# Chunk-loop stores of h2 and of the residual move from the sync queue to GpSimd's, in a one-core hybrid mLSTM and convolution layer

## The reference

```python
def step(carry, xs):                    # one chunk of 128 tokens, 4 heads
    C, n, m = carry
    ...
    P = jnp.einsum("bhld,bhsd->bhls", qc, kc) * jnp.exp(D - m_row[..., None])
    num = w_inter[..., None] * jnp.einsum("bhld,bhde->bhle", qc, C) + jnp.einsum("bhls,bhse->bhle", P, vc)
    den = w_inter * jnp.einsum("bhld,bhd->bhl", qc, n) + jnp.sum(P, axis=-1)
    h = num / jnp.maximum(jnp.abs(den), jnp.exp(-m_row))[..., None]
    ...
y = jnp.einsum("bse,ed->bsd", jnp.concatenate([y_mlstm, y_conv], axis=-1), w_out[layer])
x = x + rms_norm(y, post_mix_norm_w[layer])
h2 = rms_norm(x, pre_mlp_norm_w[layer])
a = jax.nn.relu(jnp.einsum("bsd,df->bsf", h2, w_ff1[layer]))
m_out = jnp.einsum("bsf,fd->bsd", a * a, w_ff2[layer])
x = x + rms_norm(m_out, post_mlp_norm_w[layer])
```

## Time and profile before

| | |
|---|---|
| median of three runs | 2469.12 us |
| the profiled execution | 2463.33 us, its span 2461.5 us |
| PE busy over the span | 2325.5 us (94%) |
| chunk loop, first product of q on GpSimd to the last projection | about 659 to 1001 us |
| DMA queue of SP (q1) | 190.44 MB, 132016 packets |
| GpSimd's DMA queue (q0) | 0.13 MB, 128 packets |

### The profile page before, as it was taken

How to read it: one execution, slowest core, us unless ns; L and a number is a source line. 1 busy time by engine, 2 the same in 40 slices (tenths; PEclk the granted TensorE clock), 3 DMA queues, 4 the chain that set the end, 5 groups by cost and what they waited for, 6 DMA issues and landing times.

```text
span 2461.5 us, 30415 instructions
## 1 busy us (share of the span) xinstructions
PE 2325.5 (94%) x10945; PEld 1916.1 (78%) x10945; DVE 1500.1 (61%) x2366; ACT 779.1 (32%) x1604; POOL 179.1 (7%) x98
## 2 busy tenths in 40 slices
PE   5899999999688879799999999999999999999997
PEld 3688979789677767588888888887888888888886
DVE  6889999792466656255545455454754554545546
ACT  5424333242434434332222222222422222223222
POOL 4201121111000000000000000000300000000003
PEclk8999999999899889899999999999999999999999
DMA  4011212121668767721111111115511111111113
GB/s 172 18 52 69 69 43 74 38 87 53 185 130 174 203 168 197 270 95 45 51 50 43 51 43 45 57 43 188 180 43 52 43 43 59 43 51 43 43 34 111
DMA packets 144452, 212.72 MB, mean 86 GB/s; under 512 B 7568, under 2 KB 97808, under 8 KB 144368
## 3 DMA queue, kind: packets, MB, share of 16 engines
q1 hardware_dynamic: 132016, 190.44, 25.6%
q10 hardware_dynamic: 12224, 21.04, 2.3%
q0 software_dynamic: 128, 0.13, 0.0%
HBM read 156.93 MB, written 54.66 MB: 86 GB/s over the span
## 4 chain that ended last, share of the span: by engine, by line
PE 49%; issue 29%; SPq 10%; DVE 6%; DMA 3%; ACT 1%; POOL 1%; POOLq 0%; ACTq 0%; DVEq 0%
PE psum L1472 14%; PE psum L1492 14%; PE psum L332 11%; PE psum L322 7%; SPq L923 4%; DVE c_buf L590 2%; SPq L910 2%; SPq L953 1%; SPq L912 1%; DMA winter_b<-scratch_rows 1%; PE psum L336 1%; DMA big_lo<-scratch_h_lo 1%; DVE qout L602 1%; DMA scratch_o<-th 1%; POOL acc L1454 1%
## 5 line engine op out<-in xcount | busy, mean ns | idle before, releaser
L1602 DVE TENSOR_TENSOR acc<-acc,psum 128x512 f32<-128x512 f32 x480 | 326.1, 686 | 221.5 <-PE psum L1492 218.6
L1472 PE MATMUL psum<-big_hi,w_hi 128*128 128x512 f32 x1024 | 406.3, 397 | 9.8 <-DMA big_lo<-scratch_h_lo 9.8
L1472 PE MATMUL psum<-big_lo,w_hi 128*128 128x512 f32 x1024 | 405.9, 396 | 0.0
L1472 PE MATMUL psum<-big_hi,w_lo 128*128 128x512 f32 x1024 | 405.7, 396 | 0.0
L1492 PE MATMUL psum<-w_hi,hid_hi 128*128 128x512 f32 x1024 | 399.8, 390 | 3.6 <-issue 3.6
L1492 PE MATMUL psum<-w_lo,hid_hi 128*128 128x512 f32 x1024 | 399.5, 390 | 0.0
L1492 PE MATMUL psum<-w_hi,hid_lo 128*128 128x512 f32 x1024 | 399.4, 390 | 0.0
L590 DVE SCALAR_TENSOR_TENSOR c_buf<-u_buf,par_a,c_buf 128x1024 f32<-128x1024 f32 x240 | 342.5, 1429 | 8.5 <-ACT c_buf L440 1.3
L1590 DVE TENSOR_TENSOR sq<-relu 128x512 f32<-128x512 f32 x128 | 90.6, 708 | 345.6 <-ACT relu L1525 345.6
L1472 PEld LDWEIGHTS psum<-big_hi,w_hi 128*128 128x128 f32 x1024 | 193.2, 189 | 57.2 <-issue 5.5
L1517 ACT ACTIVATE w_hi<-w_raw 128x1024 fp32r<-128x1024 f32 x64 | 64.2, 1051 | 528.8 <-PE psum L1492 528.8
(11 more groups left out here) (210 smaller groups left out, 3534.8 us busy)
## 6 DMA issues: line engine op xcount, KB each, us to landing
w_raw<-in_w SPq DMA_DIRECT2D x128, 512.0 KB, 3.5
w_raw<-in_w_in SPq DMA_DIRECT2D x25, 512.0 KB, 3.8
scratch_qk<-qout ACTq DMA_DIRECT2D x16, 512.0 KB, 2.6
x_c<-in_x SPq DMA_DIRECT2D x16, 512.0 KB, 15.8
scratch_xn<-xn SPq DMA_DIRECT2D x16, 512.0 KB, 6.4
scratch_h_hi<-h_hi SPq DMA_DIRECT2D x16, 512.0 KB, 14.9
scratch_h_lo<-h_lo SPq DMA_DIRECT2D x16, 512.0 KB, 15.6
big_hi<-scratch_h_hi SPq DMA_DIRECT2D x4, 2048.0 KB, 15.4
```

What stands on the lines that cost most here:

```text
L1472: mm = nc.tensor.matmul(psum[:, tb, :], l, r, start=kt == 0 and i == 0, stop=kt == KT - 1 and i == 2)
L1602: nc.vector.tensor_tensor(out, out, psum[:, 2 + j % 4, :], ALU.add).then_inc(sem["acc"], 1)
```

## The change

GpSimd's loop runs over 20 iterations instead of 16. In each, behind the product of q for chunk c, it waits for `h2_lo` of chunk c-4 and issues the two stores of h2, then waits for `xn` of chunk c-2 and issues its store. The sync queue loses the three stores and their waits. Its wait ahead of the token loads now asks for the first four stores of each h2 buffer (chunks 0 to 7), where it asked for those up to chunk 12. Its waits at the end of phase B (all stores landed) stay.

```diff
                     sp.wait_ge(sem["out_proj"], 2 * NCH)
                     for b in range(2):
-                        sp.wait_ge(sem["h2_out"][b], 32 * ((NCH - 3) // 2 + 1 - b))
+                        sp.wait_ge(sem["h2_out"][b], 32 * NCH // 4)
                     prefetch["tokens"](sp)
-                if c >= 4:
-                    sp.wait_ge(sem["h2_lo"], 2 * (c - 3))
-                    at = slice((c - 4) * P, (c - 3) * P)
-                    for buf, out in ((h2_hi, dram["h2_hi"]), (h2_lo, dram["h2_lo"])):
-                        sp.dma_start(out[:, :, at], buf[:, c % 2].bitcast(F32)).then_inc(sem["h2_out"][c % 2], 16)
                 if c < NCH:
                     load_x(c)
                 if c == NCH // 2:
                     prefetch["weights"](sp)
-                if 0 <= c - 2 < NCH:
-                    sp.wait_ge(sem["xn"], c - 1)
-                    sp.dma_start(dram["xn"][c - 2], xn[:, c % 2]).then_inc(sem["xn_out"][c % 2], 16)
...
-            for c in range(NCH):
-                chunk_here(pool, c)
-                if c >= 1:
-                    pool.wait_ge(sem["num"], c)
-                nc.gpsimd.tensor_tensor(qs_c[:], q_t[c % C_RING], winter_b[c % C_RING], ALU.mult).then_inc(sem["qs"], 1)
+            for c in range(NCH + 4):
+                if c < NCH:
+                    chunk_here(pool, c)
+                    if c >= 1:
+                        pool.wait_ge(sem["num"], c)
+                    nc.gpsimd.tensor_tensor(qs_c[:], q_t[c % C_RING], winter_b[c % C_RING], ALU.mult).then_inc(sem["qs"], 1)
+                if c >= 4:
+                    pool.wait_ge(sem["h2_lo"], 2 * (c - 3))
+                    at = slice((c - 4) * P, (c - 3) * P)
+                    for buf, out in ((h2_hi, dram["h2_hi"]), (h2_lo, dram["h2_lo"])):
+                        pool.dma_start(out[:, :, at], buf[:, c % 2].bitcast(F32)).then_inc(sem["h2_out"][c % 2], 16)
+                if 0 <= c - 2 < NCH:
+                    pool.wait_ge(sem["xn"], c - 1)
+                    pool.dma_start(dram["xn"][c - 2], xn[:, c % 2]).then_inc(sem["xn_out"][c % 2], 16)
```

## The result

The changed kernel takes 2480.51 us (median of 12 runs, 2473.57 to 2485.69) against 2470.4 us for the kernel before (12 runs, 2468.55 to 2477.05): ratio 1.0037, 95% interval 1.0026 to 1.0048. It is slower by 10 us, where 31 us of gain were forecast.

The account below looks back on a forecast made before the run. It took the full, in-order sync queue to feed TensorE too slowly. Terms -35.8 + 5 = -30.8 us on the profiled 2463.33 gave 2432.5, with 5.8 for the median 2438.3; range 2420 to 2476.

Parts of the forecast that it names:

- A: Rival: the DMA engines are the bound, not the queue; chunks stay at 22.4 us, total 2474 or 2469; chance 0.10.
- Do the moved stores fit beside the loads?: Chunk loop: stores, 4.7 us a chunk, fit into 11.4 us of broadcasts with idle engines; cost 0.
- Stores off the sync queue: Nine chunks from 762.07 us fall from 22.42 to 18.0 us each, 4 us given back for weight prefetch: -35.8 us.
- The chunks before 762 us ... at 0: Early chunks of the loop, ahead of the nine, left as they are: 0 us.
- Into phase C: Start of phase C: last stores, 2.5 MB, go beside the token loads; 0 to 7.5 us, 5 us taken.
- GpSimd's time: GpSimd's issuing: 4.5 us an h2 store, xn 0.5 to 1.1; 11.3 us in a chunk of 18.0, hidden.
- B: Rival: GpSimd paces part of the loop, at 7.5 us an h2 store; last stores late for weights, 2444; chance 0.08.
- C: Rival: slower, from about 8.4 us an h2 store on GpSimd's queue; at 9.5 us +32, total 2501; chance 0.16.
- The new wait in front of the product: GpSimd's loop: the next chunk's product of q stands behind the xn store; slack 2.5 us, cost 0.
- The weights: Phase C: weights are issued once all stores land; 0.9 us of slack, cost 0 at 4.5 us an h2 store.

Follow-up runs that it names:

- timed_pool: Changed kernel with each chunk's stores held on GpSimd until the next chunk's `o_c` landed, xn stored one iteration later; 2480.6 us, ratio 1.0044 to the kernel before.
- small_pool: Changed kernel with an eighth of each h2 and xn store left, phase C reading other arrays; 2437.84 us, ratio 0.9876 to the kernel before.
- tail_sp: Changed kernel with the last three h2 pairs and last xn store back on the sync queue behind the token loads; 2473.35 us, ratio 1.0021 to before.

## Why the prediction was wrong

It forecast 2438.3 us (2420 to 2476); 2480.5 was measured, and of the rivals A had the mechanism: the sign that the prediction gave for it, chunks at 22 us with `winter_b` as the releaser while GpSimd idles, is what the profile shows.

**The step that failed is "Do the moved stores fit beside the loads?", answered with cost 0.** Its two arguments were a mean (a share of 0.76 gives 17.0 us of work in a chunk) and "the engines have room while the queue doesn't", from 0.22 and 41 GB/s within the broadcasts. `timed_pool` shows that the room does not exist: stores issued there landed behind the broadcasts, and at most 0.27 of their 1.5 MB passed within them. So a chunk is a sum, of broadcasts (11.5 us) and plain transfers with the stores in them (10.9), and the sum is the same from any queue: after 13.1 + 9.4, with the stores nearly gone 12.8 + 6.7. The rule of the Trainium skill that the prediction weighed at this step (DMA: Bandwidth & Descriptors, Issuing engines are not separate DMA queues) made it 22.4 us a chunk; the trace of after agrees, with 22.46.

**"Stores off the sync queue", -35.8 us,** fell with it: 0.3 us lost over the nine chunks. The 18 us were taken from early chunks, and there they were right for a reason that I misread: the three chunks of 54.25 us had no h2, in any queue, and their broadcasts (11.9 us) and plain loads (6.2) make 18.1. The chunk of 17.54 us was not without h2, as the prediction says: the first pair was issued in it, at 749.16 us, but landed at 763.7 and 766.2, behind its broadcasts. That the issue of `x_c` ended with `winter_b`'s landing showed a full queue, but a queue behind slow transfers looks the same as one that holds idle engines up. Even with the stores gone, `small_pool` gained 2.9 us a chunk and not 4.4. TensorE's floor in a chunk was 16.54 us (16.78 taken).

**"The chunks before 762 us ... at 0"** was 7.4 us. The first pair goes out 16 us sooner, so stores that had fallen behind the loop before now fall into it, where each chunk's transfers set its time. The runs bear this out in part: these chunks take 71.8 us before, 72.4 with an eighth of the stores' bytes, 77.6 with h2 alone moved and 79.2 with all of it. No run held the first pairs back alone.

**"Into phase C", 5 us,** was 7.6: mis-sized. All the stores had landed by 1032.6 us, ahead of the tokens that TensorE waited for (1035.9 and 1046.6), and `tail_sp`, with the last stores behind the tokens, took the gap back to 28.00 us. That 7.6 is nearly the upper end of the term (2.5 MB at 335 GB/s, 7.5 us) is in part luck: the pair of chunk 13, issued 3.3 us ahead of the tokens, was still under way and is not in the 2.5 MB. The queue moved 3.15 MB in the gap; at 335 GB/s that would be 9.4 us, and the engines moved 358.

**"GpSimd's time", 4.5 us an h2 store,** was 0.87 and 0.91. Rivals B (7.5) and C (8.4 and more) fell. xn's 0.55 lay at the low end of its bounds. From 64 rows (0.54) to 1024 (0.87) the price grows by 0.33 us: most of it is per transfer. The Trainium skill's sentence on this (same page, Anatomy of one DMA, SWDGE path) holds in these rows.

**"The new wait in front of the product", cost 0,** was right: GpSimd waited for xn, the product followed 0.56 us behind the store's start, and the numerators never waited for `qs_c`. The weights too were not held up (they were issued at 1032.76 us, before at 1039.46); only the tokens were.

The last two points stand apart from the error: every part of GpSimd's own work was hidden, with room. What was lost, was lost on the transfers' side.

## What to carry to other kernels

Moving the stores to another engine's queue left the transfers' own time where it was. Before counting on such a move, ask whether the transfers that hold the loop up leave other queues through at all; a low DMA share with few GB/s can be the mark of a slow kind of transfer, not of room. Here the slow kind was the bound: laying the broadcast rows out so that each partition reads one row of 2 KB gave 3.1% with the stores on the sync queue (2392 against 2469.6 us) and 2.9% with them on GpSimd's. And the last stores lay well behind the loads of the next phase: 7.6 us were paid for bringing them forward.

## Hardware behaviour that was not expected

- 1024 reads of 512 bytes, 128 partitions reading each row, take 11.5 us, about 11 ns each; 256 of 2 KB take 2.5 to 3.0 us; 1024 of 512 bytes from different places take 1.5 to 2.5 us.
- While such reads run, packets of another queue that are issued at their start hardly pass: 0.10 of 1.5 MB in 11.2 us, at a DMA share of 0.34, and `h2_hi` landed 13.6 to 17.4 us after its issue.
- The DMA share of a stretch of broadcasts says little: 0.34 at 91 GB/s in one run, 0.99 at 81 GB/s in another.
- GpSimd issued 1024 rows in 0.85 to 0.96 us and 128 rows in 0.55, and never blocked here. ScalarE's issue of the same 1024 rows blocked for up to 9.30 us, and the sync queue's of `x_c` for 10.77.
